# Attention on TensorE: scores and projections moved between the turning of probabilities and the product with the values

## The reference

```python
def token_mixers(h, cos, sin, w_in, b_forget, w_out_a, w_out_b, w_out):
    qa, ka, va, qi, ki, wi, qb, kb, vb, fb, ga, gb = _split_cols(h @ w_in)
    ...
    # branch A: top-k keys of each query by the indexer's score, one key/value head for 8 query heads
    logit = jnp.einsum('bqhd,bqkd->bqhk', q_blk, k_sel) * ATTN_SCALE
    p = jax.nn.softmax(jnp.where(valid, logit, NEG_INF), axis=-1)
    oa = jnp.einsum('bqhk,bqkd->bqhd', p, v_sel)
    ...
    # branch B: 8 heads, causal, with a cumulative forget-gate bias
    logit = jnp.einsum('bqhd,bshd->bhqs', q_blk, kb) * ATTN_SCALE + cq - cum_t
    p = jax.nn.softmax(jnp.where(causal, logit, NEG_INF), axis=-1)
    ob = jnp.einsum('bhqs,bshd->bqhd', p, vb)
```

## Time and profile before

| | |
|---|---|
| median of 3 runs | 1828.5 us (1826.37 to 1828.74) |
| the profiled execution | 1829.64 us |
| its span | 1827.4 us |
| TensorE matmuls busy | 1676.7 us (92%) |
| VectorE, ScalarE busy | 961.7 us (53%), 496.6 us (27%) |
| attention on TensorE, L1120 first to L1145 last | about 218 to 714 us of the span |
| matmuls busy in 300 to 400 us, in 600 to 700 us | 95.3 us, 90.5 us |

### The profile page before, as it was taken

How to read it: one execution, slowest core, us unless ns; L and a number is a source line. 1 busy time by engine, 2 the same in 40 slices (tenths; PEclk the granted TensorE clock), 3 DMA queues, 4 the chain that set the end, 5 groups by cost and what they waited for, 6 DMA issues and landing times.

```text
span 1827.4 us, 22908 instructions
## 1 busy us (share of the span) xinstructions
PE 1676.7 (92%) x7928; PEld 857.0 (47%) x7929; DVE 961.7 (53%) x1913; ACT 496.6 (27%) x1020; POOL 191.1 (10%) x371
## 2 busy tenths in 40 slices
PE   5998889999998898999999999499999989999892
PEld 2563456564644555676666455233333333333330
DVE  5666697887877665556464433533333323333323
ACT  3214545454544655101110112011111111111112
POOL 0010000000000000000000000122222212222221
PEclk9999999999999999999999998699999999999996
DMA  9552201010000120112111813899999746999996
GB/s 353 184 187 67 70 19 40 24 47 1 1 1 2 58 70 1 35 34 69 34 34 70 324 58 109 328 357 398 378 327 400 283 126 233 395 401 368 397 400 246
DMA packets 102905, 316.63 MB, mean 173 GB/s; under 512 B 9920, under 2 KB 46824, under 8 KB 78256
## 3 DMA queue, kind: packets, MB, share of 16 engines
q1 hardware_dynamic: 91088, 287.88, 41.0%
q0 software_dynamic: 11744, 27.79, 6.3%
HBM read 289.14 MB, written 26.51 MB: 173 GB/s over the span
## 4 chain that ended last, share of the span: by engine, by line
PE 83%; DVE 5%; ACT 5%; DMA 4%; issue 2%; SPq 1%; POOLq 0%; POOL 0%; DVEq 0%; ACTq 0%
PE ps L1296 19%; PE ps L1222 10%; PE ps L1314 9%; PE ps L1211 6%; PE ps L1095 5%; PE ps L1257 5%; PE ps L1145 4%; PE ps L1120 4%; PE ps L1015 3%; PE ps L1159 3%; PE ps L1131 2%; PE ps L1101 2%; ACT arena L823 2%; PE ps L1053 2%; PE ps L1290 2%
## 5 line engine op out<-in xcount | busy, mean ns | idle before, releaser
L1296 PE MATMUL ps<-arena 128*64 128x512 f32 x1632 | 377.2, 605 | 17.0 <-issue 10.1
L1296 PEld LDWEIGHTS ps<-arena 128*64 128x64 f32 x1632 | 115.6, 139 | 231.7 <-issue 217.8
L1884 DVE COPY arena<-ps 128x256 f32<-128x256 f32 x51 | 21.6, 424 | 381.9 <-ACT arena L931 381.9
L1314 PE MATMUL ps<-arena 128*64 128x512 f32 x816 | 186.3, 598 | 0.6 <-DVE arena L1906 0.6
L1222 PE MATMUL ps<-rounded 128*128 128x512 f32 x768 | 183.3, 398 | 0.0
L1535 DVE TENSOR_SCALAR_CACHE_REDUCE arena<-arena,small 128x384 bf16<-128x384 f32 (+2 forms) x192 | 171.3, 939 | 0.0
L1222 PEld LDWEIGHTS ps<-rounded 128*128 128x128 f32 x768 | 144.2, 188 | 36.6 <-issue 7.7
L710 POOL DMA_INDIRECT sum_rows<-arena,ones x51 | 81.4, 1595 | 433.3 <-DVE arena L1906 422.3
L1145 PE MATMUL ps<-arena 128*64 128x128 f32 x1152 | 96.4, 286 | 23.4 <-ACT arena L823 22.4
L1211 PE MATMUL ps<-arena 128*128 128x512 f32 x256 | 112.5, 592 | 2.2 <-DVEq L1708 2.2
L1257 PE MATMUL ps<-arena 128*128 128x512 f32 x256 | 112.0, 595 | 1.9 <-DMA arena<-in_w_out_dram 1.9
(11 more groups left out here) (297 smaller groups left out, 2012.7 us busy)
## 6 DMA issues: line engine op xcount, KB each, us to landing
arena<-in_w_e_gate_dram SPq DMA_DIRECT2D x64, 1024.0 KB
arena<-in_w_e_up_dram SPq DMA_DIRECT2D x64, 1024.0 KB
arena<-in_w_e_down_dram SPq DMA_DIRECT2D x32, 2048.0 KB
arena<-in_w_mod_dram SPq DMA_DIRECT2D x12, 2048.0 KB, 8.5
arena<-in_w_in_dram SPq DMA_DIRECT2D x32, 512.0 KB, 4.5
arena<-in_x_dram SPq DMA_DIRECT2D x16, 512.0 KB, 8.4
sum_rows<-arena SPq DMA_DIRECT2D x9, 512.0 KB, 2.6
arena<-cum_rows SPq DMA_DIRECT2D x8, 512.0 KB, 5.2
```

Of the source, the lines that this page charges most:

```text
L1296: m = pe.matmul(ps[o * TB:(o + 1) * TB, 2, 0:2 * FQ].rearrange("p (j n) -> p j n", j=2), xT[:, k % NX, k // NX * TB:(k // NX + 1) * TB], w ...
L1314: m = pe.matmul(ps[o * TB:(o + 1) * TB, 5, 0:DQ], hidT[:, k % NH_T, k // NH_T * TB:(k // NH_T + 1) * TB], w_dn[c][:, k, o * DQ:(o + 1) * D ...
```

## The change

In TensorE's list alone, `scores` of unit n + 3, `pj_group`, `qa_tile`, `qa_turn` and `modulate` no longer stand as whole blocks at the start and near the end of iteration n. The scores are cut in pieces of 512 keys, a projection group and a query tile in four parts each. A new function `between(n, gap, gaps)` stands ahead of each `values(n, gap)`; `gaps` is the unit's number of groups. The four parts are spread evenly over the gaps. The pieces of the scores stand in the last gaps: one piece in the last, two in the last two (both in the only gap of a unit with one group). So the scores of unit n + 3, which were the first thing of iteration n, now come near its end. Within a gap the scores come first. The waits go with the first piece or part, and the counts with the last. The number and form of matmuls stay as they were. Before iteration 0 the order is unchanged.

```diff
-            def scores(n):
+            def score_pieces(n):
+                return (WB[UNITS[n][2]] + 511) // 512
+
+            def scores(n, piece):
...
-                pe.wait_ge(lg_done, 2 * n)
-                for a in range(0, WB[b], 512):
...
+                if piece == 0:
+                    pe.wait_ge(lg_done, 2 * n)
+                a, e = 512 * piece, min(512 * piece + 512, WB[b])
...
-            for n in range(-LEAD, N_U):
+            def between(n, gap, gaps):
+
                 if n + LEAD < N_U:
-                    scores(n + LEAD)
...
+                    last = score_pieces(n + LEAD)
+                    for piece in range(last):
+                        if max(gaps - last + piece, 0) == gap:
+                            scores(n + LEAD, piece)
+                if gap == gaps - 1 and N_B - TT < n <= N_B:
+                    qa_turn(n - (N_B - TT) - 1)
+                for part in range(4 * gap // gaps, 4 * (gap + 1) // gaps):
+                    if -3 <= n < -1:
+                        pj_piece(0, n + 7, part)
+                    elif 0 <= n < N_B - TT and n % TT in PJ_AT:
+                        pj_piece(n // TT + 1, PJ_AT[n % TT], part)
+                    elif N_B - TT <= n < N_B:
+                        qa_piece(n - (N_B - TT), part)
+                if gap == gaps - 1 and MOD_AT <= n < MOD_AT + 8:
+                    modulate(n - MOD_AT)
+
+            for n in range(-LEAD, 0):
+                between(n, 0, 1)
+            for n in range(N_U):
+                groups = len(key_groups(n))
+                turn_p(n, 0)
+                for f in range(1, groups):
                     turn_p(n, f)
...
+                    between(n, f - 1, groups)
+                    values(n, f - 1)
+                between(n, groups - 1, groups)
+                values(n, groups - 1)
```

More of the change, by code:

```diff
@@ L1086, in _, with pj_piece @@
                     m.then_inc(cumt_ps, 1)
[L1088 removed]
+            def pj_piece(p, g, part):
                 j, half = g // 2, g % 2
[L1090 to L1092 removed]
+                if part == 0:
+                    if g % 2 == 0:
+                        pe.wait_ge(wb_in[j], 16 * (p + 1))
+                    pe.wait_ge(pj_out, 6 * p + g)
                 if j < 2:
[L1094 removed]
+                    for kt in range(2 * part, 2 * part + 2):
                         m = pe.matmul(ps[:, 7, :], wB[j][:, kt, :], hT[:, kt, half * 512:(half + 1) * 512],
@@ L1097, in pj_group @@
                 else:
-                    for a in range(4):
-                        t = 4 * half + a
-                        for kt in range(KT):
-                            m = pe.matmul(ps[:, 7, a * P:(a + 1) * P], hT[:, kt, t * P:(t + 1) * P], wB[2][:, kt, :],
-                                          start=kt == 0, stop=kt == KT - 1)
-                m.then_inc(pj_ps, 1)
-            def scores(n):
+                    t = 4 * half + part
+                    for kt in range(KT):
+                        m = pe.matmul(ps[:, 7, part * P:(part + 1) * P], hT[:, kt, t * P:(t + 1) * P], wB[2][:, kt, :],
+                                      start=kt == 0, stop=kt == KT - 1)
+                if part == 3:
+                    m.then_inc(pj_ps, 1)
+            def score_pieces(n):
+                return (WB[UNITS[n][2]] + 511) // 512
+            def scores(n, piece):
                 kind, p, b = UNITS[n]
@@ L1108, in scores @@
                     q, k = raw[p % 2]
-                    if n % TT == 0:
+                    if n % TT == 0 and piece == 0:
                         pe.wait_ge(pj_out, 6 * p + 4)
@@ L1112, in scores @@
                     q, k = qaT[p // 2][:, p % 2, :], kT[:, 1, :]
-                    if n < N_B + TT:
+                    if n < N_B + TT and piece == 0:
                         pe.wait_ge(pt_copied, qa_turn_at(n - N_B) + 1)
-                pe.wait_ge(lg_done, 2 * n)
-                for a in range(0, WB[b], 512):
-                    e = min(a + 512, WB[b])
-                    for z in range(2):
-                        half = slice(z * HD, (z + 1) * HD)
-                        m = pe.matmul(ps[:, 2 * z + a // 512, 0:e - a], q[half, b * P:(b + 1) * P], k[half, a:e], start=True, stop=True)
-                m.then_inc(qk_done, 1)
+                if piece == 0:
+                    pe.wait_ge(lg_done, 2 * n)
+                a, e = 512 * piece, min(512 * piece + 512, WB[b])
+                for z in range(2):
+                    half = slice(z * HD, (z + 1) * HD)
+                    m = pe.matmul(ps[:, 2 * z + piece, 0:e - a], q[half, b * P:(b + 1) * P], k[half, a:e], start=True, stop=True)
+                if e == WB[b]:
+                    m.then_inc(qk_done, 1)
             def turn_p(n, f):
@@ L1149, in _, with qa_piece @@
             pe.wait_ge(relu_ok, N_IU)
-            def qa_tile(i):
+            def qa_piece(i, part):
                 t = TILES[i]
-                if i == 0:
+                if part == 0 and i == 0:
                     pe.wait_ge(wqa_in, 64)
                     pe.wait_ge(pj_out, 6 * PAIRS)
-                else:
+                elif part == 0:
                     pe.wait_ge(qa_tm, i)
-                for kt in range(KT):
+                for kt in range(2 * part, 2 * part + 2):
                     m = pe.matmul(ps[:, 7, :], hT[:, kt, t * P:(t + 1) * P], wqa[kt], start=kt == 0, stop=kt == KT - 1)
-                m.then_inc(qa_ps, 1)
+                if part == 3:
+                    m.then_inc(qa_ps, 1)
             def qa_turn(i):
```

21 lines of the change are left out of this document (removed).

## The result

The changed kernel takes 1891.2 us (median of 4 runs, 1890.5 to 1891.7), the kernel before 1827.4 beside it (4 runs): ratio 1.0356, 95% interval 1.0336 to 1.0376. It is slower, as forecast, but by 64 us instead of 25, and outside the range (1833 to 1868).

The account below looks back on a forecast made before the run. TensorE's list was taken to bound the attention stage. Terms -2.3 + 8.2 + 15.5 + 3 = +24.4 us on the profiled 1829.6 gave 1854.0, so a median of 1853; forecast 1843 to 1862 (0.57), 8-in-10 range 1833 to 1868.

Parts of the forecast that it names:

- The start: Before unit 3's scores: TensorE, idle there 5.8 us, can turn unit 0 and do a quarter group meanwhile; -2.3 us.
- Part 1: TensorE's own list: waits that go are mostly paid back by more changes of kind; -2.1 us per pair of heads.
- Part 2: Branch B: VectorE reads scores late, TensorE stalls 4.9 us a pair; net +2.8 a pair, +8.2 for three.
- In iterations 24 to 31 I take 0: End of branch B: a query tile in every iteration covers VectorE's lateness; -1 and +1 us cancel.
- Part 3: Branch A: late scores put VectorE's reading, `exps`, ScalarE's copy and values in series with TensorE's work; +15.5 us.
- Part 4: TensorE's clock: falls to half speed behind idle stretches cost about 1.5 us each; two falls counted, +3 us.
- a rival, 1864 to 1877: TensorE's clock falls at most stalls: 1864 us at every second of 18, 1877 at all; chance 0.13.
- other stretches of 1 to 2 us: Earlier trace of TensorE: idle stretches this long, apart from the pair shown, had no clock fall; supported counting only two.
- the lateness is absorbed: Both branches: gaps are filled and VectorE and ScalarE serve late scores in time; faster, 1814 us; chance 0.13.
- only one branch pays: Gain in one of branches A and B only: 1833 to 1843 us, chance 0.12; no change, chance 0.05.

Follow-up runs that it names:

- e1: Changed kernel with the scores whole at the iteration's start as before, keeping projection groups and query tiles in four parts; 1821.2 us, ratio 0.9952 to the kernel before.
- e8: e1 with the output copies of units 32 and 33 moved from VectorE to ScalarE; 1819.1 us, ratio 0.9937 to the kernel before.
- e9: Changed kernel plus filler matmuls nobody reads in TensorE's idle stretches, in branch A two where e4 had three; 1856.2 us, ratio 1.0151 to the kernel before.
- e12: e9 with output copies of units 32 and 33 on ScalarE, five fillers ahead of unit 34's values, none ahead of unit 33's; 1859.0 us, ratio 1.0173.
- e6: Changed kernel with scores whole and early in branch B, late and in pieces only from unit 32's on; 1864.2 us, ratio 1.0189 to the kernel before.
- e5: Changed kernel with late scores only for branch B's units, whole and early from unit 32's on; 1845.5 us, ratio 1.0085 to the kernel before.
- e4: Changed kernel plus filler matmuls nobody reads in idle stretches, one or four in branch B's, three or six in branch A's; 1867.7 us, ratio 1.0207.
- e10: e8 with seven filler matmuls added ahead of unit 3's scores; 1819.3 us, ratio 0.9949 to the kernel before.

## Why the prediction was right in sign and wrong in size

**The start, not shown.** Unit 0's first values come 2.5 us earlier than before, against my 2.3. But e1 and e8, the same kernel up to there, differ by 5.6 us at this place, so the agreement may be luck.

**Part 1, held, and e1's agreement is partly luck.** In the changed kernel iteration 8 takes 13.3 us (first turning at 326.87 to the next at 340.17) where I had 13.4, and iteration 14 takes 2.9 where I had 2.8. e1 measured -2.4 a pair against my -2.1, but 1.1 of my sum lies in iteration 14, with the scores behind the turning. In e1 the scores stay first, and from score to score that iteration takes 3.99 as before; e1's gain lies in the iterations with a projection group (0.6, 0.6, 0.3, 0.3 and 0.5 us in iterations 8 to 11 and 13), where I had less.

**Part 2, held where I worked it out.** Stalls of 3.8, 3.2 and 3.2 at units 10, 18 and 26 against 4.0, 3.1, 3.1; 1.2, 2.0 and 1.8 at n mod 8 = 5; TensorE's waits ahead of the scores are 15.8 us in 9 places, where I had some 15 in 8. With the clock held (e9), the second and third pair cost +2.5 and +2.3 against my +2.8. In the first pair (+5.2) the clock is still down for 5.4 us. "In iterations 24 to 31 I take 0" failed: +5.4, or +4.1 in e9. The pieces gained 2.7 there (e1), but the late scores cost 8.0 beside that.

**Part 3, right mechanism, term too small.** Waits of 2.1 to 2.8 us ahead of the wide units' first values, with `exps` ending just before the copy; +24.3 in e9 against my +15.5. Of the 8.8 us between them 3.3 lie in the first stretch, where I had put 3.5 for the selection; e12 shows `choose` in the chain there. How the rest divides, the fillers' own cost included, stays open. e6 shows that the loss doesn't come from branch B.

**Part 4, the step that failed.** "I take two falls, +3." The stage has 12 falls more, 65 us more at half clock. Holding the clock gave back 23.7 us of the 62.1 that the change costs between unit 0's first values and the stage's end (e9), though its fillers cost something too; the stage's busy time puts the matmuls' slowing at 29.0 us. So a term of 24 to 29 us stood in my sum as 3. I had both long stretches of the earlier trace rows before me, both followed by a fall, and set them aside for "other stretches of 1 to 2 us" of which the kernel before has only one, of 1.37 us, inside the stage. The stalls that I had predicted were of 2 to 4 us, between the 1.79 and the 5.77 that fell. I had priced this as a rival, 1864 to 1877, with the right cause at 0.13. Its 27 us for falls at every stall come near the 29.0, but by two errors that cancel: 12 falls more instead of 18, at about 2.4 us each (29.0 / 12) instead of 1.5. The rest of what the rival's 1877 lacks is mostly the 12.5 us of parts 2 and 3: e9's stage ends 33.9 later than before, the start and parts 2 and 3 gave 21.4.

The Trainium skill, page "TensorE: Matmul & The Clock Gate", section "Why this matters for your kernels", warned that idle gaps between bursts of matmuls drop the clock. The measurement goes further than that section: the gaps that it warns of are longer than the stalls of 1.8 to 2.8 us of branch A, and the clock fell behind most of these too.

**Rivals.** That the lateness is absorbed was wrong in both branches (e5, e6). That only one branch pays was wrong too.

## What to carry to other kernels

When a change turns an engine's lead into short waits for another, price the clock with the waits: on this stage the slower matmuls cost 29 us beside some 32 us of added waits. Two halves of a change that each fill or thin the same stretch can cost together what neither costs alone, as the second and third pair of heads did: split them before judging either, and take each half's cost beside the other half and not only beside the kernel before. And a wait that ends last isn't the cause if the same engine's queue holds something else as late right behind it: move the named instruction, then see whether the wait only changes its name.

## What the runs showed of the hardware

- Idle stretches of 1.8 to 2.8 us in branch A were enough for TensorE's clock to go from 2.4 to 1.2 GHz (means of 0.83 to 0.93 over stretches of 41 to 52 us): from unit 36 on, 7 of 11 such stretches of the changed kernel have a fall at them. With e9's fillers the last three stretches stayed at 2.4 GHz, though a single wait of 2.4 us was left; in e4 and e12 the clock fell at the same wait. So the length of one idle stretch alone didn't decide it.
- Seven matmuls that compute nothing, put into a wait of 5.6 us, brought eight score matmuls behind it from 2.51 to 1.35 us (e8, e10).
- Splitting a projection group into quarters among turnings and values paid, even with the changes of kind (e1: 74.7 us a pair against 77.1): they cost less than the waits that the quarters filled.
